# Latent heads: the softmax reciprocal moved from the probability rows to the output blocks

## The chip, the cores and the metric

One core of a Trainium2 chip runs the whole kernel as one program. The time is that of the device in microseconds (us), the median of several executions. TensorE (PE) multiplies matrices, VectorE (DVE) and ScalarE (ACT) work on tiles element by element, GpSimd (POOL) on tiles in SBUF, and SyncE (SP) issues the DMAs. The engines run side by side and wait for each other by semaphores.

## The reference

A two-layer decoder trunk on 1024 positions of width 1024: layer 0 mixes tokens by stick-breaking attention, layer 1 by latent attention (MLA) with 12 heads; both have 4 memory heads beside them, an output projection and a SwiGLU block. The change concerns the 12 latent heads of layer 1 alone. With q and k of 96 columns each and v of 64, they compute

```
sc = einsum('bhqd,bhkd->bhqk', q_blk, k) * scale
sc = where(key_pos <= q_pos, sc, -inf)
p  = softmax(sc, axis=-1)
o  = einsum('bhqk,bhkd->bhqd', p, v)
```

and o, heads side by side, goes into the output projection.

## The kernel before, in words

All matrix products are made of fp32r parts: each operand is split into an upper and a lower part, and a product is three matmuls (lines 84 to 86, `product3`). The latent heads are in `latent_heads` (line 2928 on), which builds one object `at_` of class `Attend`. It works on six pairs of heads. A pair is four jobs: head 0 with queries 0 to 511, head 0 with queries 512 to 1023, then head 1 in the same way. A job has four rows (tiles of 128 queries) and 4 or 8 blocks of 128 keys; a pair has 16 rows and 24 blocks, numbered tau.

For each row ("S") TensorE makes the scores in a bank pair of PSUM, with the causal mask added (line 2984); VectorE takes the negated maximum (line 1212) and multiplies it with the query's scale (line 1217); ScalarE makes the exponential into a row of SBUF, `p`, and the row's sum beside it ("P", line 1181). Then VectorE takes the reciprocal of the sum ("I", line 1226) and multiplies the row with it in place ("R", line 1232). For each block ("T") TensorE transposes up to four 128x128 tiles of the rows (line 1153) into one of two PSUM banks, ScalarE copies the upper part out (`pt_hi`, line 1193), VectorE subtracts to get the lower part (`pt_lo`, line 1237), and two blocks later ("V", `LAG` = 2) TensorE multiplies both with the values (lines 1165 and 1167). The values stand as upper and lower part side by side, so a job's output bank has 128 partitions: 64 of each part. At a job's end ("E") ScalarE copies the lower 64 out (`o_tmp`, line 1199) and VectorE adds them to the upper 64 (`o_out`, line 1243). There is one output bank, which the addition frees. SP stores the 64x512 tile (line 1258) to `attention_out_t` in DRAM, transposed: head columns in the partitions, queries along the tile.

The order of the steps is one list that all engines follow, written by `Attend.__init__` from `plan` (how many rows' scores are made by each block); the list wraps, so that the first rows of the next pair are made in the last blocks of this one. Between the steps ("X", `extras`) stands the preparation of the next pair: key and value products ("kv"), query products ("q"), norms ("ss", "rq", "ksum", "knorm"), key transposes ("kturn": `kt_hi` by ScalarE at line 3176, `kt_lo` by VectorE at line 3268), and weight splits ("wk", "wq"). VectorE's scaling of a query is line 3250, ScalarE's square of it line 3161, TensorE's sum of squares line 3347. All preparation products use one PSUM bank. The first pair is prepared in a list `OPENING` of its own. The last pair runs the list without the next pair's rows and without `extras` (`closing`), and ends in 36 filler matmuls (`keep_running`, line 92). SP loads the weights of the pair after next (lines 3021 and 3024) at a pair's start and then runs `at_.sync`, the four output stores of a pair, in order.

Of the kernel before, what the change touches and what calls it, by code (L numbers as in the profile page):

```python
# [1022 lines left out]
class Attend:  # L1023
# [8 lines left out]
    def __init__(self, nc, ctx, tag, mem, psum, k, jobs, keys_of, blocks_of, causal, scores, values, store,  # L1032
                 rows_mem, ring, score_banks, out_banks=(6, 7), plan=None, extras={}, lag=1, wrap=False, low_mem=None,
                 query_scale=None, stored=()):
# [14 lines left out]
        (self.scores_made, self.raw_max, self.nmax_done, self.exp_done, self.inv_done, self.rows_done,  # L1049
         self.turned, self.hi_done, self.split_done, self.pv_made, self.tmp_done, self.out_done) = (  # L1050
            ctx.semaphore(f"{tag}_{n}") for n in (
                "scores_made", "raw_max", "nmax_done", "exp_done", "inv_done", "rows_done", "turned",
                "hi_done", "split_done", "pv_made", "tmp_done", "out_done"))
# [11 lines left out]
        steps, made, exps, inverses, rows = [], 0, 0, 0, 0  # L1065
# [15 lines left out]
        def inverse_up_to(count):  # L1081
            nonlocal inverses
            exp_up_to(count)
            while inverses < count:
                steps.append(("I", inverses // 4, inverses % 4))
                inverses += 1

        def row_up_to(count):
            nonlocal rows
            inverse_up_to(count)  # L1090
            while rows < count:
                steps.append(("R", rows // 4, rows % 4))
                rows += 1

        score_up_to(plan[0])
        row_up_to(plan[0])
# [16 lines left out]
        row_up_to(plan[-1])  # L1113
# [3 lines left out]
        self.closing = [s for s in steps if s[0] not in "SPIR" or s[1] < self.nj] + (rest if wrap else [])  # L1117
# [19 lines left out]
    def pe(self, pe, steps, turn=0, extra=None, ready=None, values_ready=None):  # L1137
        for kind, *step in steps:
# [2349 lines left out]
```

## Time and profile before

| | us |
|---|---|
| three runs | 2627.41, 2628.19, 2633.21 |
| median | 2628.19 |
| the profiled execution | 2629.66 |
| its span, first to last instruction | 2627.90 |
| TensorE busy | 2526.2 (96%) |
| VectorE busy | 1739.8 (66%) |
| ScalarE busy | 1310.6 (50%) |
| GpSimd busy | 1112.5 (42%) |

The latent heads take the span's part from about 1482 to 1890 us. An engine's busy time counts its own instructions alone. Matmuls are pipelined, so their durations overlap: a 512-wide one is shown with 0.39 us and the next starts 0.23 us later. "Idle" in square brackets is the engine's gap just before an instruction, with the instruction of another engine that ended it. "PEclk" is the clock granted to TensorE, 1.00 for 2.4 GHz and 0.50 for 1.2 GHz.

### The profile page before, as it was taken

What the parts mean: (1) busy time and instruction counts of PE and PEld (TensorE: products, weight loads), DVE (VectorE), ACT (ScalarE), POOL (GpSimd) and SP (SyncE); (2) the same over time, 40 slices, a digit from 0 to 9 for tenths busy, and PEclk for the clock granted to TensorE, in tenths of its full rate; (3) what the DMA queues carried; (4) which work ended last, traced back from release to release, by engine and by line L of the source; (5) the groups of instructions that cost most, each with busy time, mean ns of one, the idle gap of its engine ahead of it and who ended that gap; (6) DMA issues with size and microseconds to landing.
All of it is one profiled execution on the core that took longest, in us unless ns stands there. A gap on an engine that the chain in (4) does not pass through costs nothing. (4 is left out here: it accounts for less than half of the span.)

```text
span 2627.9 us, 37382 instructions
## 1 busy us (share of the span) xinstructions
PE 2526.2 (96%) x12150; PEld 2057.7 (78%) x12150; DVE 1739.8 (66%) x2659; ACT 1310.6 (50%) x2483; POOL 1112.5 (42%) x839
## 2 busy tenths in 40 slices
PE   7999999999999999999989999999899999999999
PEld 6867777667888888888777777778687888888887
DVE  6767787855765666478655377777648665665595
ACT  6567777745433333444655366666545333333443
POOL 2134454311465566555411332332003665565554
PEclk9999999999999999999999999999899999999999
DMA  4111110153222232674302000000242322234843
GB/s 145 45 29 33 33 33 9 33 176 113 81 100 104 100 112 88 228 240 148 107 21 59 14 20 22 21 21 21 83 166 90 116 100 104 100 112 143 285 125 117
DMA packets 182796, 242.76 MB, mean 92 GB/s; under 512 B 31376, under 2 KB 105872, under 8 KB 182672
## 3 DMA queue, kind: packets, MB, share of 16 engines
q1 hardware_dynamic: 182672, 241.19, 27.7%
q8 instruction: 68, 1.11, 0.2%
q14 instruction: 56, 0.46, 0.1%
HBM read 175.60 MB, written 65.54 MB: 92 GB/s over the span
## 5 line engine op out<-in xcount | busy, mean ns | idle before, releaser
L2385 POOL TENSOR_TENSOR l0s_run_lo<-l0s_run,l0s_run_hi 128x512 fp32r<-128x512 f32 (+2 forms) x120 | 143.5, 1195 | 215.6 <-DVE l0s_run_hi L2538 215.6
L477 POOL TENSOR_TENSOR l1f_wd_lo<-l1f_d,l1f_wd_hi 128x512 fp32r<-128x512 f32 x77 | 108.0, 1403 | 104.6 <-ACT l1f_wd_hi L552 104.6
L477 POOL TENSOR_TENSOR l0f_wd_lo<-l0f_d,l0f_wd_hi 128x512 fp32r<-128x512 f32 x77 | 109.3, 1422 | 97.2 <-ACT l0f_wd_hi L552 97.0
L84 PE MATMUL banks<-l1f_T_hi,l1f_op_hi 128*128 128x512 f32 x352 | 137.1, 390 | 1.1 <-DVE l1f_T_lo L697 1.1
L84 PE MATMUL banks<-l0f_T_hi,l0f_op_hi 128*128 128x512 f32 x352 | 137.1, 390 | 1.0 <-DVE l0f_T_lo L697 1.0
L85 PE MATMUL banks<-l0f_T_lo,l0f_op_hi 128*128 128x512 f32 x352 | 137.0, 389 | 0.0
L85 PE MATMUL banks<-l1f_T_lo,l1f_op_hi 128*128 128x512 f32 x352 | 136.9, 389 | 0.0
L86 PE MATMUL banks<-l1f_T_hi,l1f_op_lo 128*128 128x512 f32 x352 | 136.9, 389 | 0.0
L86 PE MATMUL banks<-l0f_T_hi,l0f_op_lo 128*128 128x512 f32 x352 | 136.9, 389 | 0.0
L439 POOL TENSOR_TENSOR l1f_s<-l1f_raw 128x512 f32<-128x512 f32 x44 | 66.6, 1513 | 158.1 <-DMA l1f_raw<-in_w_ffn_gu_dram 135.3
L509 ACT ACTIVATE l1f_op_hi<-l1f_s 128x512 fp32r<-128x512 f32 x88 | 55.2, 631 | 140.4 <-PE banks L86 140.4
L509 ACT ACTIVATE l0f_op_hi<-l0f_s 128x512 fp32r<-128x512 f32 x88 | 55.2, 631 | 140.4 <-PE banks L86 140.4
L462 POOL TENSOR_TENSOR l1f_hid<-l1f_c,l1f_gate 128x512 f32<-128x512 f32 x44 | 67.5, 1535 | 129.6 <-DVE l1f_c L719 129.6
L462 POOL TENSOR_TENSOR l0f_hid<-l0f_c,l0f_gate 128x512 f32<-128x512 f32 x44 | 67.0, 1524 | 129.5 <-DVE l0f_c L719 129.5
L84 PE MATMUL banks<-ht_hi,l0s_w_hi 128*128 128x512 f32 x288 | 119.6, 415 | 1.4 <-DVE l0s_q L2033 1.2
L84 PE MATMUL banks<-l0f_wd_hi,l0f_a_hi 128*128 128x512 f32 x308 | 120.0, 390 | 0.6 <-DVE l0f_a_lo L760 0.6
L439 POOL TENSOR_TENSOR l0f_s<-l0f_raw 128x512 f32<-128x512 f32 x44 | 66.5, 1512 | 127.0 <-DMA l0f_raw<-in_w_ffn_gu_dram 102.9
L1237 DVE TENSOR_TENSOR l1aa_pt_lo<-banks,l1aa_pt_hi 128x512 fp32r<-128x512 f32 (+2 forms) x144 | 78.8, 554 | 62.3 <-ACT l1aa_pt_hi L1193 61.9
L86 PE MATMUL banks<-l0f_wd_hi,l0f_a_lo 128*128 128x512 f32 x308 | 119.8, 389 | 0.0
L85 PE MATMUL banks<-l0f_wd_lo,l0f_a_hi 128*128 128x512 f32 x308 | 119.8, 389 | 0.0
L84 PE MATMUL banks<-l1f_wd_hi,l1f_a_hi 128*128 128x512 f32 x308 | 119.8, 389 | 0.0
L85 PE MATMUL banks<-l1f_wd_lo,l1f_a_hi 128*128 128x512 f32 x308 | 119.8, 389 | 0.0
(536 smaller groups left out, 8456.1 us busy)
## 6 DMA issues: line engine op xcount, KB each, us to landing
l0f_raw<-in_w_ffn_gu_dram SPq DMA_DIRECT2D x22, 1024.0 KB, 5.0
l1f_raw<-in_w_ffn_gu_dram SPq DMA_DIRECT2D x22, 1024.0 KB, 4.9
l0f_a_raw<-hidden_rows SPq DMA_DIRECT2D x77, 256.0 KB, 3.9
l1f_a_raw<-hidden_rows SPq DMA_DIRECT2D x77, 256.0 KB, 3.4
hidden_rows<-l0f_hid SPq DMA_DIRECT2D x44, 256.0 KB, 2.0
l0f_d<-in_w_ffn_down_dram SPq DMA_DIRECT2D x44, 256.0 KB, 4.9
hidden_rows<-l1f_hid SPq DMA_DIRECT2D x44, 256.0 KB, 2.0
l1f_d<-in_w_ffn_down_dram SPq DMA_DIRECT2D x44, 256.0 KB, 4.8
```

The costliest lines, as they stand in the source:

```text
L84: pe.matmul(out, l_hi, r_hi, start=first, stop=False, skip_group_check=True)
L85: pe.matmul(out, l_hi, r_lo, start=False, stop=False, skip_group_check=True)
L86: return pe.matmul(out, l_lo, r_hi, start=False, stop=last, skip_group_check=True)
L439: pool.tensor_tensor(out[:], left, right, op).then_inc(s_made, 1)
L462: pool.tensor_tensor(hidden(q), cs[q][:], gate[q][:], ALU.mult).then_inc(hid_done, 1)
L477: pool.tensor_tensor(wd_lo[g % RING][:], held[HELD_AT[DOWN[p][1]]][i][:], as_f32(wd_hi[g % RING][:]), ALU.subtract).then_inc(wd_lo_done, 1)
L509: act.activation(op_hi[n][:], stationary(n, b), ACT.Copy).then_inc(op_hi_done, 1)
L1237: dve.tensor_tensor(self.pt_lo[tau % self.np][:, c0:HALF], self.t_ps[tau % 2][:, c0:HALF], as_f32(self.pt_hi[tau % self.np][:, c0:HALF]), ...
L2385: pool.tensor_tensor(run_lo[x % NR][:, f:HALF], run[x % NR][:, f:HALF], as_f32(run_hi[x % NR][:, f:HALF]), ALU.subtract).then_inc(run_spli ...
```

## The change

The probability rows stay unscaled. The four sums of a job are inverted in one instruction (128x4) after the first score of the next job, SP stores them to a DRAM tensor `row_scales` as 512 values in the order of the queries, and loads that row back into 64 partitions (`o_scale`). At a job's end VectorE adds the two parts of the output as before, into `o_sum`, and then multiplies with `o_scale` into `o_out`. The transposes wait for the exponentials and no longer for the scaled rows. `rsum`, `rinv`, `o_scale` and `o_out` have two buffers each. The first two jobs' scales are sent (`first_scales`) ahead of the second pair's weights; later SP's order is, for job n: store its reciprocals, store the output of job n - 2, load its scales.

```diff
-        self.nmx, self.rsum, self.rinv, self.raw_nmx = (low_mem(f"{tag}_{n}", [P, 4])
-                                                        for n in ("nmx", "rsum", "rinv", "raw_nmx"))
-        self.o_tmp = mem(f"{tag}_o_tmp", [HD, HALF])
-        self.o_out = [mem(f"{tag}_o_out{s}", [HD, HALF]) for s in range(2)]
+        self.nmx, self.raw_nmx = (low_mem(f"{tag}_{n}", [P, 4]) for n in ("nmx", "raw_nmx"))
+        self.rsum, self.rinv = ([low_mem(f"{tag}_{n}{s}", [P, 4]) for s in range(2)] for n in ("rsum", "rinv"))
+        parts, both = mem(f"{tag}_parts", [P, HALF]), [mem(f"{tag}_out_scale{s}", [P, HALF]) for s in range(2)]
+        self.o_tmp, self.o_sum = parts[0:HD, :], parts[HD:2 * HD, :]
+        self.o_out, self.o_scale = [t[0:HD, :] for t in both], [t[HD:2 * HD, :] for t in both]
...
         def score_up_to(count):
             nonlocal made
             while made < count:
                 exp_up_to(made)
-                row_up_to(made - 1)
                 steps.append(("S", made // 4, made % 4))
                 made += 1
+                if made % 4 == 1 and made > 4:
+                    steps.append(("I", made // 4 - 1))
...
-                row_up_to(max(rows, 4 * n + 4))
-                inverse_up_to(exps - 1)
+                exp_up_to(max(exps, 4 * n + 4))
                 steps.append(("T", n, j, tau))
...
-                pe.wait_ge(self.rows_done, turn * self.ns + 4 * n + 4)
+                pe.wait_ge(self.exp_done, turn * self.ns + 4 * n + 4)
...
+                if i == 0 and (n >= 2 or not (isinstance(turn, int) and turn == 0)):
+                    act.wait_ge(self.inv_done, turn * self.nj + n - 1)
...
-                dve.reciprocal(self.rinv[:, one], self.rsum[:, one]).then_inc(self.inv_done, 1)
-            elif kind == "R":
-                n, i = step
-                s = 4 * n + i
-                one, row = slice(s % 4, s % 4 + 1), self.p[n % self.ring][i]
-                dve.wait_ge(self.inv_done, turn * self.ns + s + 1)
-                dve.tensor_scalar(row[:], row[:], self.rinv[:, one], None, ALU.mult).then_inc(self.rows_done, 1)
+                n = step[0]
+                dve.wait_ge(self.exp_done, turn * self.ns + 4 * n + 4)
+                if n >= 2 or not (isinstance(turn, int) and turn == 0):
+                    dve.wait_ge(self.scale_stored, 16 * (turn * self.nj + n - 1))
+                dve.reciprocal(self.rinv[n % 2][:], self.rsum[n % 2][:]).then_inc(self.inv_done, 1)
...
                 dve.wait_ge(self.tmp_done, turn * self.nj + n + 1)
+                dve.tensor_tensor(self.o_sum, self.o_ps[n % len(self.o_ps)][0:HD, :], self.o_tmp, ALU.add).then_inc(self.out_done, 1)
+                dve.wait_ge(self.out_done, 1 + turn * self.nj + n + 1)
                 dve.wait_ge(self.stored[n % 2], 16 + 16 * (turn * (self.nj // 2) + n // 2))
-                dve.tensor_tensor(self.o_out[n % 2][:], self.o_ps[n % len(self.o_ps)][0:HD, :], self.o_tmp[:],
-                                  ALU.add).then_inc(self.out_done, 1)
+                dve.wait_ge(self.scale_in[n % 2], 16 * (turn * (self.nj // 2) + n // 2 + 1))
+                dve.tensor_tensor(self.o_out[n % 2], self.o_sum, self.o_scale[n % 2], ALU.mult).then_inc(self.out_scaled, 1)
...
+    def store_scale(self, sp, n, turn=0):
+        sp.wait_ge(self.inv_done, turn * self.nj + n + 1)
+        with self.nc.allow_non_contiguous_dma("row scales"):
+            sp.dma_start(self.scale_dram[n % self.nj].rearrange("(i p) -> p i", p=P), self.rinv[n % 2][:]).then_inc(self.scale_stored, 16)
+
+    def load_scale(self, sp, n, turn=0):
+        sp.wait_ge(self.scale_stored, 16 * (turn * self.nj + n + 1))
+        sp.dma_start(self.o_scale[n % 2], self.scale_dram[n % self.nj].partition_broadcast(HD)).then_inc(self.scale_in[n % 2], 16)
...
+    def first_scales(self, sp):
+        for n in range(2):
+            self.store_scale(sp, n)
+            self.load_scale(sp, n)
+
+    def sync(self, sp, turn=0, last=False):
+        for n in range(2, self.nj if last else self.nj + 2):
+            self.store_scale(sp, n, turn)
+            self.store_out(sp, n - 2, turn)
+            self.load_scale(sp, n, turn)
+        if last:
+            for n in range(self.nj - 2, self.nj):
+                self.store_out(sp, n, turn)
...
             load(1)
+            at_.first_scales(sp)
             with sp.Fori(0, PAIRS - 2) as g:
                 load(g + 2)
                 at_.sync(sp, g)
```

## Rows read from the trace of the kernel before

**Rows 1.** Busy time by stretch: us, each engine (x instructions), granted clock, DMA, GB/s

```profile
1500.00:1540.00 40.00, 34.93 (x208) 29.27 (x205) 28.09 (x68) 23.56 (x57) 15.22 (x15) 1.00 0.09 22
1540.00:1840.00 300.00, 284.63 (x1689) 236.94 (x1688) 237.14 (x570) 199.31 (x468) 82.96 (x86) 1.00 0.08 20
1840.00:1895.00 55.00, 43.00 (x222) 35.73 (x221) 36.30 (x79) 28.04 (x58) 1.27 (x1) 0.81 0.16 49
```

**Rows 2.** TensorE's waits, 1540 to 1840: us in total, times, longest

```profile
PE banks L3347 <- DVE l1a_kt_lo L3268: 4.5, 5, 1.0
PE banks L3347 <- ACT l1a_q_sq L3161: 3.5, 5, 0.7
PE banks L3364 <- DVE l1a_kt_lo L3268: 2.5, 5, 0.5
PE banks L84 <- ACT l1aa_p L1181: 2.3, 4, 0.6
```

**Rows 3.** Groups, 1500 to 1895: busy us, mean ns of one, idle before

```profile
L1232 DVE TENSOR_SCALAR l1aa_p<-l1aa_p,l1aa_rinv 128x128 f32<-128x128 f32 (+3 forms) x96 | 53.8, 565 | 2.3
...
L1243 DVE TENSOR_TENSOR l1aa_o_out<-banks,l1aa_o_tmp 64x512 f32<-64x512 f32 x24 | 16.3, 679 | 1.5 <-ACT l1aa_o_tmp L1199 1.2
...
L1226 DVE RECIPROCAL l1aa_rinv<-l1aa_rsum 128x1 f32<-128x1 f32 x96 | 14.7, 153 | 3.3 <-ACT l1aa_p L1181 3.3
...
L3244 DVE TENSOR_TENSOR l1a_k<-l1a_k,l1a_rk 128x512 f32<-128x512 f32 x11 | 7.6, 692 | 0.4
```

**Rows 4.** Timeline of a middle pair: start us, us, instruction, idle before

```profile
1770.18 0.74 DVE L3268 SCALAR_TENSOR_TENSOR l1a_kt_lo<-banks,l1a_gcol,l1a_kt_hi 128x512 fp32r<-128x512 f32 x1
...
1770.97 1.08 PE L3347 MATMUL banks<-l1a_q_sq,l1a_ones 128*64 128x512 f32 x4 [0.98 <-DVE l1a_kt_lo L3268]
```

**Rows 5.** Timeline, second block of a pair

```profile
1785.69 0.67 DVE L3250 TENSOR_TENSOR l1a_q<-banks,rope_table 128x512 f32<-128x512 f32 x1
```

**Rows 6.** Timeline, end of the opening

```profile
1527.11 2.53 DVE L1232 TENSOR_SCALAR l1aa_p<-l1aa_p,l1aa_rinv 128x1024 f32<-128x1024 f32 x2
...
1530.39 0.41 PE L1153 MATMUL banks<-ident,l1aa_p 128*128 128x128 f32 x2 [1.91 <-DVE l1aa_pt_lo L1237]
```

**Rows 7.** Timeline, start of the last pair

```profile
1846.10 0.93 DVE L1232 TENSOR_SCALAR l1aa_p<-l1aa_p,l1aa_rinv 128x1024 f32<-128x1024 f32 x2
...
1847.78 0.66 PE L1153 MATMUL banks<-ident,l1aa_p 128*128 128x128 f32 x2 [2.79 <-DVE l1aa_pt_lo L1237]
```

**Rows 8.** Timeline, last pair, before its last two jobs' blocks

```profile
1870.26 0.19 ACT L1181 ACTIVATION_READ_ACCUMULATOR l1aa_p<-banks,l1aa_nmx,l1a_rq 128x1 f32 x1
...
1870.28 0.47 PE L1165 MATMUL banks<-l1aa_pt_hi,l1a_v 128*128 128x512 f32 x1 [2.24 <-DVE l1aa_pt_lo L1237]
...
1872.22 1.11 PE L1153 MATMUL banks<-ident,l1aa_p 128*128 128x128 f32 x4 [0.66 <-DVE l1aa_p L1232]
```

**Rows 9.** Busy time and granted clock in stretches of the last pair and the opening

```profile
1843.55:1847.80 4.25, 0.71 (x6) 0.64 (x6) 3.53 (x13) 3.63 (x8) 0.00 (x0) 0.94 0.00 0
1847.80:1854.10 6.30, 5.95 (x24) 5.28 (x25) 2.87 (x7) 2.33 (x7) 1.27 (x1) 0.50 0.60 191
1867.80:1871.30 3.50, 1.26 (x8) 0.74 (x6) 3.43 (x8) 2.69 (x6) 0.00 (x0) 0.98 0.00 0
1871.30:1881.20 9.90, 8.44 (x32) 6.84 (x32) 4.45 (x10) 3.69 (x7) 0.00 (x0) 0.50 0.11 26
1527.00:1530.50 3.50, 1.59 (x8) 1.01 (x8) 3.47 (x5) 1.38 (x3) 3.50 (x3) 1.00 0.07 26
```

**Rows 10.** DMA issues: count, KB each, median us from issue to landing

```profile
attention_out_t<-l1aa_o_out SPq DMA_DIRECT2D x24, 128.0 KB, 2.2
...
l1m_mcol<-in_ln_mem_dram SPq DMA_DIRECT2D x1, 4.0 KB, 3.8
...
l0m_gcol<-in_ln_attn_dram SPq DMA_DIRECT2D x1, 4.0 KB, 12.6
```

**Rows 11.** Timeline, end of the stage

```profile
1884.30 4.51 PE L92 MATMUL banks<-strict,ident_r 128*128 128x256 f32 x36
```

More of the change, by code:

```diff
@@ L1064, in __init__ @@
                           for j in range(blocks_of(half))]
-        steps, made, exps, inverses, rows = [], 0, 0, 0, 0
+        steps, made, exps = [], 0, 0
         def score_up_to(count):
@@ L1079, in exp_up_to @@
                 exps += 1
[L1081 to L1093, printed above, removed]
         score_up_to(plan[0])
-        row_up_to(plan[0])
+        exp_up_to(plan[0])
         self.opening, steps = steps, []
@@ L1112, in __init__ @@
             steps += rest
-        row_up_to(plan[-1])
+        exp_up_to(plan[-1])
         self.steps = steps
         self.first_steps = [s for s in steps if s[0] not in "VE" or s[1] >= 0]
-        self.closing = [s for s in steps if s[0] not in "SPIR" or s[1] < self.nj] + (rest if wrap else [])
+        self.closing = [s for s in steps if s[0] not in "SPI" or s[1] < self.nj] + (rest if wrap else [])
     def product(self, tau):
@@ L1253, in begin, with store_out @@
             sp.sem_inc(s, 16)
-    def sync(self, sp, turn=0):
-        for n, (h, half) in enumerate(self.jobs):
-            sp.wait_ge(self.out_done, 1 + turn * self.nj + n + 1)
-            sp.dma_start(self.store(h, half, turn), self.o_out[n % 2][:]).then_inc(self.stored[n % 2], 16)
+    def store_scale(self, sp, n, turn=0):
[5 more added lines that the diff above has]
+        sp.dma_start(self.o_scale[n % 2], self.scale_dram[n % self.nj].partition_broadcast(HD)).then_inc(self.scale_in[n % 2], 16)
+    def store_out(self, sp, n, turn=0):
+        h, half = self.jobs[n]
+        sp.wait_ge(self.out_scaled, turn * self.nj + n + 1)
+        sp.dma_start(self.store(h, half, turn), self.o_out[n % 2]).then_inc(self.stored[n % 2], 16)
+    def first_scales(self, sp):
[10 more added lines that the diff above has]
+                self.store_out(sp, n, turn)
     def stores(self, turns):
@@ L2925, in _, with latent_heads @@
             last.then_inc(ss_made, 1)
-def latent_heads(nc, tag, k, w_q_up, w_kv_up, g_k, cq, ckv, table, k_rot, k_ss, q_eps, at, psum, ot_dram, passage, w_out, stored, opening):
+def latent_heads(nc, tag, k, w_q_up, w_kv_up, g_k, cq, ckv, table, k_rot, k_ss, q_eps, at, psum, ot_dram, scale_dram, passage, w_out, stored, opening):
     mem = Memory(nc, at, 229344)
@@ L2989, in latent_heads @@
                      lambda h, half, g: ot_dram[bass.ds(g * P + h * HD, HD), half * HALF:(half + 1) * HALF],
-                     low, 4, psum["pair"], (6,), plan, extras, LAG, True, mem, lambda h, tile: rq[:, NS * h + tile:NS * h + tile + 1], stored)
+                     low, 4, psum["pair"], (6,), plan, extras, LAG, True, mem, lambda h, tile: rq[:, NS * h + tile:NS * h + tile + 1], stored, scale_dram)
         sem = lambda n: ctx.semaphore(f"{tag}_{n}")
@@ L3052, in _ @@
             load_passage(sp, passage, w_out, ot_dram, passage_in)
-            at_.sync(sp, PAIRS - 1)
+            at_.sync(sp, PAIRS - 1, True)
             sp.wait_ge(passage_in, 64)
@@ L3457, in build @@
                 heads_count = latent_heads(nc, f"{tag}a", k, a["mla_w_q_up"][0], a["mla_w_kv_up"][0], a["mla_g_kn"][0],
-                             cq, ckv, table, k_rot, k_ss, q_eps, mem.at, psum, ot_dram, passage, a["w_out"][layer], kept[6:8], opening)
+                             cq, ckv, table, k_rot, k_ss, q_eps, mem.at, psum, ot_dram, scale_dram, passage, a["w_out"][layer], kept[6:8], opening)
             project_and_swiglu(nc, f"{tag}f", k, x, x_dram, x_att, a_dram, ot_dram, a["w_out"][layer], a["ln_ffn"][layer],
```

20 lines of the change are left out of this document (10 added, 10 removed).

## The prediction

> **What bounds the kernel now.** I read the busy table of the stage that the change touches first, by stretches. The twelve latent heads run as six pairs, from 1500 to 1890 us. In 1540 to 1840 (five pairs less a little) TensorE is busy 284.63 of 300 us, VectorE 237.14, ScalarE 199.31 [rows 1]. So TensorE sets the pace, and all that a lighter VectorE can give there is TensorE's idle time, 15.4 us in all. The opening (1500 to 1540) has 5.1 us of it, the last stretch (1840 to 1895) 12.0 us, and only the last runs at a mean granted clock of 0.81 [rows 1].
>
> Next the list of waits, to see how much of the idle time ends on VectorE. In 1540 to 1840 TensorE waited 4.5 us for the split of the keys (kt_lo), 3.5 us for the squared queries, 2.5 us again for kt_lo and 2.3 us for an exponential that frees a score bank [rows 2]: 12.8 of the 15.4 us, or about 2.6 us a pair. Two of the four end directly on VectorE, the other two stand one step behind it (the exponential needs the row maximum, the square needs the scaled query).
>
> The groups of instructions then say what the change takes away. Scaling the probability rows costs VectorE 53.8 us in 96 instructions, the 96 reciprocals 14.7 us [rows 3].
>
> **The change part by part.**
>
> *VectorE's load.* Removed: 53.8 us of row scaling, and 96 reciprocals of 153 ns become 24, so 72 x 0.153 = 11.0 us. Added: one multiplication of 64x512 per job, 24 in all. The trace has none like it. The nearest rows are the addition that it follows, 64x512 in 679 ns, and a multiplication of two tiles in SBUF, 128x512 in 692 ns [rows 3]; I take 0.69 us, plus 0.08 for waiting on its own engine's addition, so 24 x 0.77 = 18.5 us. The upper bound is the slowest case beside GpSimd's work that I saw: a pair of row scalings (1024 and 128 wide) took 2.53 us in the opening [rows 6] and 0.93 us where GpSimd was idle [rows 7], 1.6 us more, which would make it 2.3 us. The lower bound is half a full-width operation, 0.35 us, if partitions counted. Net, VectorE loses 53.8 + 11.0 - 18.5 = 46 us, nearly 8 us a pair. None of that is time by itself, since TensorE sets the pace; it counts only where TensorE waits.
>
> *The transposes' new wait.* They waited for the scaled rows and now wait for the exponentials, one VectorE step earlier. ScalarE's and TensorE's order of work does not change; ScalarE's new wait, for a reciprocal two jobs back, is met long before.
>
> *Middle pairs (five).* I took the stalls one at a time. The longest: a row's scaling (565 ns by the mean of all widths [rows 3]) stands in front of the row maximum that delays kt_lo to 1770.18, and TensorE stands 0.98 us [rows 4]. Without it kt_lo starts 0.3 to 0.6 us earlier: take 0.4. The other kt_lo stall (0.5 us a pair) has a scaling in front in the same way: it goes. The stall on the exponential (2.3 / 4 = 0.57 us) has one in front too: 0.45. The one on the squared query (0.7 us) lies behind VectorE work that stays: half, 0.35. The small stall at a bank that the output addition frees: 0.15. That is 1.85 us a pair. What is late next: in the second block of a pair the multiplication now stands between the output addition and the scaling of a query (0.67 us, at 1785.69 [rows 5]); the query's square follows, 0.6 us on ScalarE, and then the key product that takes its bank. The path has about 0.3 us to spare, so some 0.4 us of new stall. And 0.25 us a pair for stalls that only move to the next wait. 1.85 - 0.4 - 0.25 = 1.2 us a pair, 6.0 us for five. Bounds: 0 (all moves on) and 2.6 us a pair (13 us).
>
> *Opening.* At the start of the first block the two scalings of 2.53 us hold back the splits, and TensorE stands 1.91 us at 1530.39 [rows 6]. Without them the first split follows its upper part directly, before TensorE has run out of query products: all 1.9 us. The other gaps there belong to the chain of the query norms, of which VectorE's rows are a small part: 0.3. Together 2.2 us; bounds 1.0 and 3.0.
>
> *Last pair.* Here TensorE has no preparation of a next pair to fill with. At its start two scalings (0.93 us) stand before the splits, and TensorE idles 2.79 us to 1847.78 [rows 7]. Without them the splits follow ScalarE's two exponentials and its upper parts, 1.1 us earlier; a shorter stall just ahead gives 0.4. Later TensorE idles 2.24 us to 1870.28. The row names the split, but the product also needs the output bank, which the output addition (0.67 us) freed just before. Of this only 0.35 us of that is the scaling of a row, the rest is the maximum of the last 1024-wide row. Then the transposes wait for the last row's scaling until 1872.22, though its exponential was read out at 1870.26 + 0.19 [rows 8]. They now queue only behind the two products before them, and start near 1870.9: 1.3 us with the 0.35. Sum 1.1 + 0.4 + 1.3 = 2.8, less 0.1 for the multiplication in front of a later split: 2.7 us. Bounds 1.5 and 4.
>
> *The clock in the last pair.* It fell to its lower level (0.50, 1.2 GHz) twice: for 6.3 us from 1847.8 and for 9.9 us from 1871.3. Ahead of the falls TensorE was busy 0.71 of 4.25 us and 1.26 of 3.50 us; in a stretch of the opening with 1.59 of 3.50 us it stayed at 2.4 GHz [rows 9]. Without the removed waits the first stretch would hold about 1.7 us idle at a time, less than the opening's 1.91; the second still about 1.9. So I expect the first fall to go (chance 0.65) and the second to go or shorten in half the cases. Worth: in the first stretch TensorE was busy 5.95 us, at double rate 3.0, but the split chain takes part of it: 2.0 us. In the second the blocks came every 1.7 us and would come every 0.95 (one upper part of 0.6 and one split of 0.69 us, two banks deep): 3.2 us. I put 2.0 + 1.0 = 3.0 us into the sum; bounds 0 and 5.2. The Trainium skill (TensorE: Matmul & The Clock Gate, Terms) prices a throttled stretch at its length times the missing share of the clock; by that rule the two stretches cost 3.2 and 4.9 us, and the sum would be 5.1 us larger. The rows speak for less, since in such a stretch TensorE also waits for the splits.
>
> *The trip through DRAM.* Per job a store of 512 separate 4-byte values and a load of 512 values into each of 64 partitions, both on SP's queue. The nearest rows: a load of 1024 single values landed after 3.8 us [rows 10], output stores of the same 128 KB as the new load after 2.2 us; with two issues of 0.5 us, 7 us. The slowest small load of the page, behind other traffic, took 12.6 us [rows 10]: 16 us as the upper bound. A job's sums are complete at the first score of the next job, its product ends eight or more blocks later: at least 20 us in the middle pairs, about 11 us for the third job of the last pair. So it is hidden. SP waits longer before it stores an output tile, which nobody waits for within that time. The weights of the second pair are issued behind the first two trips, 7 us later, near 1532, and are used after 1542. The Trainium skill speaks against this edit (DMA: Bandwidth & Descriptors, Rules for kernel authors: a strided last dimension becomes one descriptor per element, and should be rearranged). It changes no number here, because the trip's length is covered.
>
> *End of the stage.* The last output tile is ready 0.8 us later. TensorE's 36 filler products run from 1884.30 to 1888.81 [rows 11], and the next stage starts only behind them; the addition ended at 1885.8, so 3 us of cover: nothing.
>
> **Sum.** 6.0 + 2.2 + 2.7 + 3.0 = 13.9 us. The profiled execution took 2629.66 us (span 2627.9 and 1.8 around it), so 2615.8. It lay 1.5 us above the median of the three runs, 2628.19, so I predict 2614.3.
>
> **Rivals.**
> A. *The clock does not come back* (both gaps are still long enough, or fall so that they count). For it: the second gap stays near 1.9 us. Against it: the opening's row. Gain 13.9 - 3.0 = 10.9 us: 2617.3.
> B. *The waits only move.* TensorE is already 95% busy in the middle pairs, and each stall has ScalarE's work behind it too (exponential, upper part, square). The middle gives 0 to 1, opening and last pair 2 to 3: about 2624.
> C. *The multiplication lies on the path*: slower. VectorE runs in order, so at each job's end the next split or row maximum waits 0.77 us more; if TensorE follows each time, 24 x 0.77 = 18.5 us against 13.9 gained, or 2633. It decides from 0.58 us exposed per job. Against it: four jobs a pair lose 16 scalings in exchange, and the splits have slack of a block in most places.
> D. *The scales come too late*: a trip of over 20 us stalls VectorE, and behind it TensorE. At 25 us, 5 us for each of some 20 jobs: +86 us, 2714. No row is near.
>
> **How the numbers follow.** Forecast (gain 9 to 20 us, with one or both falls of the clock gone or shortened): 0.60. A: 0.17. B: 0.16. C: 0.05. D: 0.02. Single runs of this kernel differ by up to 0.2% (5.3 us), about what can be told from no change. Half of B gains less than that, and a fifth of C loses less. Faster by over 0.2%: 0.60 + 0.17 + 0.08 = 0.85; within: 0.08 + 0.01 = 0.09; slower: 0.04 + 0.02 = 0.06. Range: A and most of B are inside, and the upper bounds of middle and clock at the low end: 2606 to 2623.5.
>
> **What would show it.** Row scalings gone, 24 reciprocals of 128x4, 24 multiplications of 0.69 us. VectorE's busy time in the stage down by some 46 us. In the list of waits kt_lo and the exponential at half their times; the gap at the start of the first block gone; the transposes of the last job starting right after the products before them; mean clock of the last stretch above 0.9. VectorE never waiting for a landed scale. Wrong would be: a multiplication well over 0.7 us, a new wait of the key product for the squared query over 0.5 us a pair, or the same clock in the last stretch.

## The result, and the profile after

The changed kernel takes 2640.95 us (median of 6 runs, 2636.28 to 2644.97), the one before 2627.78 (6 runs beside them, 2624.93 to 2633.21). The ratio is 1.0049, 95% interval 1.0035 to 1.0063: 0.5% slower, where 0.5% faster was predicted. The profiled execution took 2642.17 us with a span of 2640.4, which is 12.5 us more than the span before.

To place these 12.5 us I cut the stage at instructions that every kernel of this study has: VectorE's first memset (the stage starts), ScalarE's copies of the upper half of the output (one per job, 24 in all), and ScalarE's first instruction of the next stage. "Opening" runs to the first copy, "five pairs" to the 21st, "last pair" to the 24th. All in us. The four columns of the stage come from one execution of each kernel, the profiled one; the medians are of all runs. The kernel before was timed again beside each group of experiments, and its medians there lie between 2629.2 and 2631.0, so kernels of different groups are best compared by their ratios. The cut "last pair" leaves out the first 11 us or so of the last pair, which fall under "five pairs". In "multiply, no trip" two memsets of the ones stand ahead of the instruction that is taken as the start.

| kernel | opening | five pairs | last pair | stage | median |
|---|---|---|---|---|---|
| before | 55.21 | 316.99 | 30.11 | 407.89 | 2627.78 |
| after | 55.50 | 323.44 | 34.96 | 419.58 | 2640.95 |
| rows unscaled only | 54.60 | 307.52 | 25.80 | 393.52 | 2613.04 |
| multiply, no trip | 51.87 | 322.84 | 27.41 | 407.73 | 2629.99 |
| trip, no multiply | 55.40 | 312.64 | 35.16 | 408.87 | 2628.93 |
| compact store | 55.55 | 322.59 | 27.43 | 411.25 | 2632.17 |
| multiply deferred | 55.30 | 310.11 | 37.23 | 408.32 | 2628.76 |
| compact, strided read | 53.05 | 331.25 | 27.36 | 417.34 | 2637.60 |
| deferred and compact | 53.05 | 308.69 | 28.90 | 396.32 | 2617.41 |
| GpSimd multiplies | 53.05 | 312.59 | 27.74 | 399.04 | 2619.57 |
| behind next split, compact | 54.59 | 315.15 | 28.14 | 403.55 | 2628.94 |
| pair-crossing one deferred | 55.50 | 316.87 | 36.56 | 414.61 | 2632.83 |

So 11.7 of the 12.5 us lie in this stage: 6.45 in the five pairs, 4.85 in the last one. The busy table of the changed kernel, to be held against [rows 1] (us, each engine's busy time, granted clock, DMA share, GB/s):

```profile
1500.00:1540.00 40.00, 35.77 (x202) 29.68 (x201) 20.85 (x48) 24.30 (x58) 15.42 (x16) 0.96 0.03 4
1540.00:1840.00 300.00, 278.24 (x1646) 231.49 (x1645) 217.51 (x446) 190.25 (x453) 80.81 (x86) 1.00 0.14 31
1840.00:1895.00 55.00, 39.73 (x224) 33.18 (x223) 35.02 (x70) 30.87 (x66) 2.58 (x2) 0.88 0.21 50
```

In 1540 to 1840 VectorE has 20 us less to do and TensorE, which should have gained from it, stands 6.4 us longer. TensorE's waits in that stretch (us in total, times, longest), against [rows 2]:

```profile
PE banks L3359 <- DVE l1a_kt_lo L3280: 6.0, 4, 1.5
PE banks L84 <- ACT l1a_q_sq L3173: 5.9, 4, 1.5
PE banks L3359 <- ACT l1a_q_sq L3173: 4.0, 5, 1.2
PE banks L84 <- ACT l1a_v L3165: 2.4, 5, 0.5
PE banks L1154 <- DVE l1aa_parts L1228: 1.7, 8, 0.5
PE banks L3376 <- ACT l1a_q_sq L3173: 1.3, 4, 0.4
```

The wait for an exponential is gone, as forecast, and so is the second one for kt_lo. The second line is new and is the largest change: a key product (line 84) waits 1.5 us in each pair for a squared query. The third job's end has the same chain in front of the key transposes (the last line). The first line, 4.5 us before, and the third, 3.5 before, have grown. The second block of a pair shows where it comes from (start us, duration, engine, instruction, idle before it):

```profile
1595.88 0.69 DVE L1228 TENSOR_TENSOR l1aa_parts<-banks,l1aa_parts 64x512 f32<-64x512 f32 x1
...
1596.45 1.28 POOL L3073 TENSOR_TENSOR l1a_v<-l1a_v,l1a_v 128x512 fp32r<-128x512 f32 x1 [10.04 <-ACT l1a_v L3201]
...
1596.81 1.47 DVE L1232 TENSOR_TENSOR l1aa_out_scale<-l1aa_parts,l1aa_out_scale 64x512 f32<-64x512 f32 x1 [0.25 <-DVE l1aa_parts L1228]
...
1598.31 0.69 DVE L3262 TENSOR_TENSOR l1a_q<-banks,rope_table 128x512 f32<-128x512 f32 x1
...
1599.12 0.60 ACT L3173 ACTIVATE l1a_q_sq<-banks 128x512 f32<-128x512 f32 x1 [2.74 <-DVE l1a_q L3262]
...
1599.77 0.38 PE L84 MATMUL banks<-l1a_wk_hi,ckv_hi 128*128 128x256 f32 x1 [1.47 <-ACT l1a_q_sq L3173]
```

Read it backwards: TensorE idles 1.47 us for the square; the square started when the query was scaled; the scaling stood behind the new multiplication, which waited 0.25 us for VectorE's own addition and then took 1.47 us where the same instruction takes 0.69 us in three jobs of four. A subtraction of GpSimd runs from 1596.45 to 1597.73, and the multiplication ends 0.55 us behind it. The kernel before had this to spare at the same place:

```profile
1785.69 0.67 DVE L3250 TENSOR_TENSOR l1a_q<-banks,rope_table 128x512 f32<-128x512 f32 x1
1786.48 0.60 ACT L3161 ACTIVATE l1a_q_sq<-banks 128x512 f32<-128x512 f32 x1 [1.04 <-DVE l1a_q L3250]
...
1787.34 0.33 PE L84 MATMUL banks<-l1a_wk_hi,ckv_hi 128*128 128x256 f32 x1
```

The square ended at 1787.08, 0.26 us before the key product. The multiplication puts in 0.25 + 1.47 = 1.72 us, and 1.72 - 0.26 = 1.46 is the wait that is measured. The Trainium skill has the mechanism (SBUF — State Buffer, SBUF: two separate sides): a VectorE instruction with two inputs in SBUF and a GpSimd instruction that reads SBUF exclude each other, and whichever starts first holds the shared ports to its end. The trace agrees.

In the last pair the time goes to one wait:

```profile
1871.15 0.38 SPq L1246 DMA_DIRECT2D row_scales<-l1aa_rinv  x1
...
1882.31 0.45 SPq L1250 DMA_DIRECT2D l1aa_out_scale<-row_scales  x1
...
1882.81 0.59 SPq L1246 DMA_DIRECT2D row_scales<-l1aa_rinv  x1
...
1883.75 0.69 DVE L1228 TENSOR_TENSOR l1aa_parts<-banks,l1aa_parts 64x512 f32<-64x512 f32 x1
...
1890.85 0.69 DVE L1232 TENSOR_TENSOR l1aa_out_scale<-l1aa_parts,l1aa_out_scale 64x512 f32<-64x512 f32 x1 [6.42 <-DMA l1aa_out_scale<-row_scales]
...
1892.41 1.09 PE L1142 MATMUL banks<-ident,l1aa_p 128*128 128x128 f32 x4 [6.24 <-DVE l1aa_pt_lo L1223]
```

The scales of the third job leave at 1871.15; the load behind them can only be issued at 1882.31, when the store has landed, and VectorE goes on 8.5 us later. The trip takes 19.7 us. Most trips of this trace take about 13 us from store to landed load, with a load of 2.7 to 5.2 us; in three of 24, of which this is the last, the load takes 8.1 to 9.8 us. All three loads have the next job's store, 512 single numbers, issued 0.5 to 2 us behind them, but four others with such a store 0.6 us behind landed after 2.7 to 2.8 us. So that store alone is not the reason, and what makes three of the loads long is open; with the compact store (below) none took over 4.1 us. VectorE stands for 6.42 us, behind it the splits, behind them TensorE. The clock in this stretch (columns as above):

```profile
1876.00:1886.20 10.20, 6.76 (x34) 5.27 (x32) 5.86 (x11) 5.88 (x13) 0.00 (x0) 0.83 0.20 27
1886.20:1892.40 6.20, 0.00 (x0) 0.02 (x1) 1.52 (x3) 0.15 (x1) 0.00 (x0) 0.72 0.03 0
1892.40:1898.00 5.60, 5.59 (x25) 4.50 (x26) 2.43 (x5) 1.95 (x5) 0.00 (x0) 0.71 0.14 47
```

The groups of 1500 to 1900, against [rows 3] (busy us, mean ns of one, idle before):

```profile
L1208 DVE TENSOR_TENSOR l1aa_nmx<-l1aa_raw_nmx,l1a_rq 128x1 f32<-128x1 f32 x96 | 31.0, 323 | 5.0
...
L1232 DVE TENSOR_TENSOR l1aa_out_scale<-l1aa_parts,l1aa_out_scale 64x512 f32<-64x512 f32 x24 | 20.4, 849 | 9.6 <-DMA l1aa_out_scale<-row_scales 6.4 <-DVE l1aa_parts L1228 2.8
...
L1218 DVE RECIPROCAL l1aa_rinv<-l1aa_rsum 128x4 f32<-128x4 f32 x24 | 4.2, 176 | 4.2 <-ACT l1aa_p L1172 1.9 <-issue 1.5 <-DMA row_scales<-l1aa_rinv 0.8
```

### The profile page after: what moved, and what is told of

Same layout as the page of the kernel before. It is cut to its first block and busy times, and to the rows that moved or that the text cites. A ratio compares the mean times of both kernels' runs of the same rounds, so it can differ in the third digit from the quotient of the medians.

```text
span 2640.4 us, 37367 instructions
## 1 busy us (share of the span) xinstructions
PE 2524.9 (96%) x12150; PEld 2056.4 (78%) x12150; DVE 1718.0 (65%) x2515; ACT 1310.1 (50%) x2483; POOL 1112.3 (42%) x839
## 3 DMA queue, kind: packets, MB, share of 16 engines
q1 hardware_dynamic: 197264, 244.39, 28.1%
## 5 line engine op out<-in xcount | busy, mean ns | idle before, releaser
L86 PE MATMUL banks<-l1f_wd_hi,l1f_a_lo 128*128 128x512 f32 x308 | 119.8, 389 | 0.0
```

Of the source, the lines that this page charges most:

```text
L86: return pe.matmul(out, l_lo, r_hi, start=False, stop=last, skip_group_check=True)
```

## The experiments

All were timed over five rounds beside the kernel before. In the first four kernels one part each is taken out of the change. The edits are cut to the lines that matter; "..." marks what is left out.

**Rows unscaled only.** The rows are no longer scaled, and the output is not normalised at all: no multiplication, no trip.

```diff
-                dve.tensor_tensor(self.o_sum, self.o_ps[n % len(self.o_ps)][0:HD, :], self.o_tmp, ALU.add).then_inc(self.out_done, 1)
-                dve.wait_ge(self.out_done, 1 + turn * self.nj + n + 1)
                 dve.wait_ge(self.stored[n % 2], 16 + 16 * (turn * (self.nj // 2) + n // 2))
-                dve.wait_ge(self.scale_in[n % 2], 16 * (turn * (self.nj // 2) + n // 2 + 1))
-                dve.tensor_tensor(self.o_out[n % 2], self.o_sum, self.o_scale[n % 2], ALU.mult).then_inc(self.out_scaled, 1)
+                dve.tensor_tensor(self.o_out[n % 2], self.o_ps[n % len(self.o_ps)][0:HD, :], self.o_tmp, ALU.add).then_inc(self.out_done, 1)
...
```

> Leaves the normalisation out: rows unscaled, no multiplication of the output block, no trip through DRAM; the reciprocals (24 of 128x4) stay. Theory Q (the removed row scaling does give what was forecast without the clock; the multiplication in VectorE's queue and the trip cost more): 8 to 14 us below before, about 2617. Theory M (waits only move, ScalarE's and TensorE's own order bound the pairs): 0 to 4 us below before, 2624 to 2628; the intervals between the same job ends of successive middle pairs stay at 63.5 to 63.9 us, while by Q they fall to about 62.

Measured: 2613.04 us (2609.51 to 2618.22), ratio 0.9943 [0.9930, 0.9957]. A pair takes 62.2 us instead of 63.8, and the "last pair" of the table 25.8 instead of 30.1. Removing the row scaling is worth what was forecast for the whole change; everything that is lost comes from what was put in its place.

**Multiply, no trip.** The multiplication stays, by a tile of ones written once; the output is not normalised.

```diff
-                dve.wait_ge(self.scale_in[n % 2], 16 * (turn * (self.nj // 2) + n // 2 + 1))
...
+            for t in at_.o_scale:
+                dve.memset(t, 1.0)
```

> As the changed kernel, but the output blocks are multiplied with a constant tile of ones, and no reciprocal goes to DRAM. Theory Q1 (the multiplication stands in front of the scaling of a query, and with two SBUF operands it waits for GpSimd): middle pairs as in the changed kernel, 65.7 us from job end to job end, the 1.5 us wait of the key product for the squared query still there; the last pair's 6.2 us stall gone: 2633 to 2636. Theory Q2 (the trip's small packets and SP's order cost the middle pairs too): middle pairs back at 63.7 or less, 2622 to 2627.

Measured: 2629.99 us, ratio 1.0002 [0.9992, 1.0011]. The multiplication alone costs 17 us over the kernel without it: 15.3 in the five pairs, 1.6 in the last. A middle pair takes 65.4 us, close to theory Q1's 65.7, and the key product's 1.5 us wait is there; the total lies below Q1's range and above Q2's. Of the 1.6 us, 1.4 lie between the second and the third output copy, where the granted clock is 0.72 in the mean, against 1.00 without the multiplication.

**Trip, no multiply.** Store, load and VectorE's wait for the load stay; the addition writes the output block itself, the multiplication is a copy of one column, and the output is not normalised.

```diff
-                dve.tensor_tensor(self.o_out[n % 2], self.o_sum, self.o_scale[n % 2], ALU.mult).then_inc(self.out_scaled, 1)
+                dve.tensor_copy(self.o_sum[:, 0:1], self.o_scale[n % 2][:, 0:1]).then_inc(self.out_scaled, 1)
```

> As the changed kernel, but the output block isn't multiplied (one column of the loaded scales is copied instead, so that VectorE's wait for them stays). Theory Q1: middle pairs at 62 to 64 us, the 6 us stall in the last pair stays: 2622 to 2630. Theory Q2: middle pairs at 65 to 66, 2636 to 2641.

Measured: 2628.93 us, ratio 0.9997 [0.9986, 1.0008]. The last pair takes 35.16 us, 9.4 more than with neither, and a middle pair about 63 us; both this and the total lie where theory Q1 put them. The five pairs take 5.1 us more too; yet with the multiplication in place the trip adds only 0.6 there (323.44 against 322.84). The two costs don't add up in the middle pairs, and which of wait, copy and traffic makes the 5.1 us was not separated.

**Compact store.** The scales are stored as 128 runs of 16 bytes; they reach the wrong queries.

```diff
-            sp.dma_start(self.scale_dram[n % self.nj].rearrange("(i p) -> p i", p=P), self.rinv[n % 2][:])...
+            sp.dma_start(self.scale_dram[n % self.nj].rearrange("(p i) -> p i", i=4), self.rinv[n % 2][:])...
```

> As the changed kernel, but the reciprocals are stored with the four values of a partition side by side in DRAM (128 runs of 16 bytes in place of 512 of 4), which gives the scales to the wrong queries. If the store's 10 us come from the number of runs, it falls to 3 to 4 us, the next load lands in under 4 us too, and the last pair's wait of 6.4 us for a landed scale goes: 6 us below the changed kernel, 2635. If the time is the round trip of any small store, nothing moves: 2641.

Measured: 2632.17 us, ratio 1.0008 [0.9996, 1.0020]. The last pair takes 27.43 us, as without any trip; the middle pairs don't move (65.6 us against 65.7). The median is 8.8 us below the changed kernel's, where 6 were expected. SP's wait for its store in 1500 to 1895 (us in total, times, longest), in the changed kernel:

```profile
SPq L1250 <- DMA row_scales<-l1aa_rinv: 159.3, 21, 10.2
```

and with the compact store:

```profile
SPq L1250 <- DMA row_scales<-l1aa_rinv: 11.9, 19, 1.7
```

With the multiplication in place, the trip costs nothing in either part once it is short (322.59 and 27.43 us, against 322.84 and 27.41 without a trip). It left the question of why 24 multiplications cost 17 us.

**Multiply deferred.** The multiplication gets a step of its own at the end of the block.

```diff
                 steps += [("X", x) for x in extras.get(tau, ())]
+                steps += [("M", s[1]) for s in self.product(tau - lag)[1:]]
```

> The multiplication of a job stands behind the extras of its block in VectorE's order, not right behind the addition; all else as changed. Theory (it costs time because of where it stands: at the second block of a pair it is ahead of the query scaling, on which TensorE's key product waits): the stretch from one pair's last output copy to the next pair's first falls from 9.85 to about 8.4 us, a middle pair from 65.7 to about 64.2, the last pair stays near 35 (the trip is not touched), total about 2631. Rival (VectorE's busy time bounds these stretches, wherever the multiplication stands): a middle pair stays at 65.7, total about 2640.

Measured: 2628.76 us (12 runs), ratio 0.9992 [0.9977, 1.0007]. The direction is the theory's, the size is not: a middle pair takes 62.35 us, 3.3 less, not 1.5. The stretches between the four output copies of a pair went from 24.86, 10.48, 20.48 and 9.86 us to 24.09, 10.46, 19.60 and 8.19: three of the four places had a price, not one. The second block was only the one that showed as a single long wait. (Of the five intervals between the pairs' first copies, the first and the fourth take 63.19 and 63.03 us.) The last pair still has its long wait for the scales, 9.1 us in this trace, and takes 37.23 us, 2.3 more than in the changed kernel; why it is longer was not followed.

**Compact, strided read.** A store in 16-byte runs that is right for each query: the multiplication reads the scales with a step of four numbers.

```diff
+                four = lambda t: t.rearrange("d (i p) -> d i p", p=P)
+                dve.tensor_tensor(four(self.o_out[n % 2]), four(self.o_sum),
+                                  self.o_scale[n % 2].rearrange("d (p i) -> d i p", i=4), ALU.mult)...
```

> The scales are stored as 128 runs of 16 bytes and loaded as they lie; the multiplication reads them with a step of four numbers, so that each query gets its own. Theory (the last pair lost its time to the store of 512 single numbers): the last pair falls from 35.0 to about 27.4 us, a middle pair stays at 65.6, total about 2632, as in the run with the compact store. Rival (reading one of two inputs with a step of 16 bytes slows the multiplication, say to 1.4 us each, 4 a pair on the path as the plain one is): a middle pair at 67 to 68 us, total 2640 to 2645.

Measured: 2637.60 us (2635.57 to 2642.39), ratio 1.0036 [1.0023, 1.0049]. The last pair fell as expected, but the rival's size came true in the middle, 68.0 us a pair (the total lies between the two forecasts). The first of its multiplications:

```profile
1535.39 1.09 DVE L1233 TENSOR_TENSOR l1aa_out_scale<-l1aa_parts,l1aa_out_scale 64x512 f32<-64x512 f32 x1
```

1.09 us in place of 0.69, and 1.85 in place of 1.46 beside GpSimd's subtraction. The Trainium skill (SBUF — State Buffer, Door 1: The DMA port swizzle) says that full rate needs a second access within the same 16 bytes; here each number of the scales lies in another 16, and the trace agrees. A multiplication longer by 0.4 us, four times a pair, made the pair 2.35 us longer: where it stands, each microsecond of it costs more than one.

**Deferred and compact.** The last two edits together.

> Both edits together: the multiplication behind the block's extras, the compact store with the strided read. Theory (two independent losses): middle pair 64.2, last pair 27.4, total about 2623, faster than the kernel before by 0.2 to 0.3%. Rival (VectorE's time bounds, place does not matter): about 2632, no difference from the compact store alone.

Measured: 2617.41 us (2613.08 to 2623.90), ratio 0.9962 [0.9946, 0.9977]. It computes all that the change computes and is 0.4% faster than the kernel before, where the changed kernel is 0.5% slower. A middle pair takes 62.4 us, against 62.2 with no multiplication at all, though three of a pair's four now take 1.08 us and the fourth 1.36. The last pair takes 28.9 us, 3.1 more than with none; 2.1 of them lie between its second and third copy, at a mean granted clock of 0.75 against 1.00. Both theories' totals were too high. The same place as above:

```profile
1586.17 1.28 POOL L3078 TENSOR_TENSOR l1a_v<-l1a_v,l1a_v 128x512 fp32r<-128x512 f32 x1 [10.02 <-ACT l1a_v L3206]
1586.32 0.69 DVE L3267 TENSOR_TENSOR l1a_q<-banks,rope_table 128x512 f32<-128x512 f32 x1
...
1587.04 1.35 DVE L1236 TENSOR_TENSOR l1aa_out_scale<-l1aa_parts,l1aa_out_scale 64x512 f32<-64x512 f32 x1
1587.12 0.60 ACT L3178 ACTIVATE l1a_q_sq<-banks 128x512 f32<-128x512 f32 x1 [1.03 <-DVE l1a_q L3267]
```

The query scaling, which reads one input from PSUM, runs at its usual 0.69 us beside GpSimd; the square starts right behind it, and the stretched multiplication has nobody behind it. TensorE's waits in 1540 to 1840, with the key product's gone:

```profile
PE banks L3364 <- DVE l1a_kt_lo L3285: 5.2, 5, 1.2
PE banks L3364 <- ACT l1a_q_sq L3178: 3.5, 5, 0.7
PE banks L1143 <- DVE l1aa_pt_lo L1224: 2.3, 2, 2.1
```

**GpSimd multiplies.** Compact store; the multiplication is four more steps of GpSimd, which waits for its own instruction before and behind each.

```diff
-    POOL_ORDER = ("v1", "ksq 0", "ksq 1", "krot 0", "qlo 0", "qlo 1", "krot 1", "qlo 2", "wq 0", "wq 1", ...
+    POOL_ORDER = ("v1", "m -1", "ksq 0", "m 0", "ksq 1", "krot 0", "qlo 0", "qlo 1", "krot 1", "m 1", "qlo 2", "wq 0", "m 2", "wq 1", ...
```

> The compact store, and the multiplication moved from VectorE to GpSimd, which does it between its own subtractions and waits for its instruction before and behind it; the addition of a job waits until the job before is multiplied. Theory (what costs is VectorE's part of the multiplication, with the wait for its own addition ahead of it): a middle pair falls to about 62.5 to 63, as without the multiplication, total about 2618 to 2620. Rival (GpSimd's multiplication, over 1.3 us each, holds VectorE up while it runs, or delays GpSimd's subtractions on which key products wait): a middle pair at 65 us or above, total 2630 or above.

Measured: 2619.57 us (2617.76 to 2621.16), ratio 0.9963 [0.9950, 0.9976]; a middle pair 63.5 us. The total is the theory's, the middle pair half a microsecond above its range. The group of its multiplications in 1540 to 1840:

```profile
L1239 POOL TENSOR_TENSOR l1aa_out_scale<-l1aa_parts,l1aa_out_scale 64x512 f32<-64x512 f32 x18 | 27.8, 1546 | 73.9 <-DVE l1aa_parts L1230 48.0 <-issue 24.6 <-POOL l1a_v L3080 1.1
```

1.55 us each, against 1.08 for VectorE's with the same read, and yet the five pairs are only 5.1 us longer than without any multiplication (312.59 against 307.52), a third of what VectorE's 0.69 us cost right behind the addition. This run takes the work off VectorE and changes its place at once, so it does not tell the two apart.

**Behind next split, compact.** As deferred and compact, but the multiplication stands behind the split of the next block.

```diff
                 steps.append(("T", n, j, tau))
+                steps += [("M", s[1]) for s in self.product(tau - lag - 1)[1:]]
```

> As the run with both edits (deferred multiplication, compact store), but the multiplication stands one step later still: behind the split of the next block, not ahead of it. Theory (in the last pair, where no extras lie between, the multiplication still delays that split: its last pair took 28.9 us against 25.8 with no multiplication at all): middle pair stays at 62.4, the last pair falls to about 27, total about 2615.5. Rival (what is left in the last pair is the state of the clock or the longer strided read, not the place): last pair stays at 28 to 29, total 2617 to 2618.

Measured: 2628.94 us (12 runs), ratio 0.9996 [0.9985, 1.0008]. This theory fell: the last pair gave 0.8 us, not 1.9, and at 28.1 lies where the rival put it, with a mean clock of 0.73 between its second and third copy, where it was 0.75 before this edit and 1.00 with no multiplication. The middle pairs lost 1.3 each (63.7 us), in three of the four stretches. The traces say in whose way the multiplication now is. It starts just ahead of a subtraction of GpSimd twice a pair, and these take 1.38 and 2.12 us where they take 1.04 and 1.42 alone: here GpSimd is the one that waits. TensorE's waits grow from 5.2 to 9.0 us for kt_lo, and from 0.7 to 3.1 for the output addition (all of 1540 to 1840). Which of the two begins the loss is not shown.

**Pair-crossing one deferred.** Of the four multiplications of a pair only the one in the second block of the next pair is deferred; store and load as changed.

```diff
+                steps += [("M", s[1]) for s in self.product(tau - lag)[1:] if s[1] == -1]
```

> Only the multiplication of a pair's fourth job, which falls into the second block of the next pair, is deferred behind that block's extras; the three others and the trip stay as changed. Theory (each place has its own price, 1.66 us here, 0.8 and 0.9 at the first and third job, nothing at the second, as the stretches of the run with all four deferred show against the changed kernel): a middle pair at 64.0, total about 2633 to 2634. Rival (the 3.3 us a pair come from this place alone, by what it sets off in later blocks): a middle pair at 62.4, total as with all four deferred, 2629.

Measured: 2632.83 us (12 runs), ratio 1.0010 [0.9999, 1.0021]; a middle pair 64.0 us. The theory holds. Each place has its own price: 1.65 us here, and 24.85 and 20.47 us in the stretches behind the first and third job's copies, untouched by this edit.

## Why the prediction was wrong, by its own steps

*Row scaling removed: right in sum, not in its parts.* Without multiplication and trip the kernel gained 14.4 us in the stage. The forecast without what it took off for the multiplication (2.0 and 0.1) is 16.0, of which the clock in the opening hid some. The middle pairs gave about 1.65 us each, where the stalls of [rows 2] and [rows 4] promised 1.6 (1.85 less 0.25). But the longest stall, from which 0.4 us a pair was to come, did not move; with the rows unscaled only it still reads

```profile
PE banks L3348 <- DVE l1a_kt_lo L3269: 4.5, 5, 1.1
```

as before. The waits for the exponential and the second one for kt_lo went whole. That the sum came out is in part luck.

*Opening: right, and hidden by the clock.* Forecast 2.2 us. In the kernel with deferred multiplication and compact store it is 55.21 - 53.05 = 2.16. The 13 us from 40 to 53 us behind the stage's start, first in the kernel before:

```profile
1522.19:1535.19 13.00, 11.02 (x69) 9.30 (x68) 9.49 (x22) 6.78 (x17) 6.66 (x7) 1.00 0.17 43
```

then in the deferred and compact kernel, where the 1.91 us of [rows 6] is gone:

```profile
1518.06:1531.06 13.00, 12.92 (x85) 11.42 (x84) 6.79 (x17) 8.05 (x21) 6.53 (x8) 1.00 0.32 76
```

and in the changed kernel's profiled execution, as free of gaps, but at a granted clock of 0.88:

```profile
1523.90:1536.90 13.00, 12.92 (x71) 11.11 (x70) 6.06 (x17) 7.43 (x19) 7.13 (x7) 0.88 0.07 12
```

Such a fall stands in seven of the eleven traces without row scaling (mean clock of their openings 0.92 to 0.94; 0.97 or 0.98 in the other four and in the one trace of before). So it may belong to the change and not to chance; no run decides it.

*The multiplication in the middle pairs: the step that failed.* The prediction said that its path "has about 0.3 us to spare, so some 0.4 us of new stall", in one of a pair's four jobs, and nothing in the others: 2.0 us in all. It measured 15.3 us, 3.1 a pair. The 0.3 us to spare was right, though no row was given for it: it is 0.26. Three errors are in the rest. The instruction was taken as 0.77 us, with 0.08 for the wait that no row shows and that measures 0.22 to 0.25; in the job that counts it was 0.25 + 1.47, because GpSimd was at work, although the bound of 2.3 us had been read off just such a case [rows 6] and was used for the load only, not for the stall. The third job's end has the same query scaling behind it and was not looked at. And the first job's end has a price of 0.8 us as well, by a chain that I did not follow. That the place makes most of the price is shown: deferred by a few instructions, the same multiplications leave a middle pair at 62.35 us against 62.2 (the five pairs at 310.1 against 307.5, the long store included). GpSimd's part is smaller: it makes one multiplication of four 0.78 us longer (1.47 less 0.69), by estimate 0.8 of the 3.1 us a pair. The prediction had named this failure among its signs, a new wait of the key product for the squared query over 0.5 us a pair; it is 1.5.

*Last pair and clock: near in sum, wrong in its parts.* Forecast 2.8 + 3.0 = 5.8 us without the multiplication. The prediction thought that the first fall of the clock would go (0.65) and that the second might. With the rows unscaled only it was the other way round. The gap at the start of the last pair shrank from 2.79 to 2.06 us, not to 1.7, and the fall behind it stayed:

```profile
1831.93:1833.99 2.06, 0.00 (x1) 0.03 (x1) 1.01 (x3) 2.04 (x7) 0.00 (x0) 0.99 0.00 0
1834.00:1840.60 6.60, 6.25 (x25) 5.58 (x26) 2.89 (x7) 3.05 (x8) 1.27 (x1) 0.50 0.64 209
```

None of the eleven traces without row scaling is free of it (mean clock 0.53 to 0.75 between the fourth copy of the fifth pair and the first of the last). The second fall went whole, and with it the table's "last pair" gave 4.3 us. The start gave about 1.2 us, the excess of the fifth of the five intervals (2.8) over a middle pair's 1.65, where 1.5 of waits and 2.0 of clock were forecast. The multiplication was priced at 0.1 us there and cost 1.6, mostly because the second fall comes back with it (0.72 against 1.00, above). In the changed kernel the stretch from 1840 to 1895 ran at 0.88, below the 0.9 that was named as a sign.

*The trip: the second step that failed.* Forecast 7 us, upper bound 16, covered everywhere. It took 13 us in most jobs and 19.7 us where it mattered. The nearest row chosen [rows 10] was a load of single numbers in 3.8 us; a store of single numbers took about 10. The forecast's own cover for the third job of the last pair, 11 us, was below its own upper bound, and that was the place to stop. The stall cost 7.55 us (34.96 - 27.41). The sentence of the Trainium skill that spoke against this edit (DMA: Bandwidth & Descriptors, Rules for kernel authors: one descriptor per element of a strided last dimension) was cited and set aside as covered; the last pair was decided by it. The trace agrees with it: packets under 512 bytes grew by 13056, and by 3840 with 16-byte runs. The weights behind the first two trips are those of the third pair, not the second; they went out at 1539.52 where 1532 was forecast, and no wait of TensorE for them is in the lists.

*VectorE's load.* Forecast 46 us less. By the groups: -53.8 for the rows, -10.5 for the reciprocals, +20.4 for the multiplications, and +6.9 on the small multiplications that make the maxima (24.1 before, 31.0 after). -37 us. The 6.9 are GpSimd's: in the kernel before 20 of the 96 started while GpSimd was at work and took 11.9 us together, in the changed one 19 did and took 18.7, and the others took 0.16 each in both. And -37 is the sum of the records, which overlap each other a little. The time in which VectorE ran anything, from the stage's start to its last output copy, fell from 301.8 to 278.6 us, by 23: half of what was forecast. A sum of records overstates what an engine is freed of.

*The account.* Forecast -13.9, measured +11.7 in the stage, 25.6 apart: multiplication in the five pairs 13.3, in the last 1.5; trip 7.55 and 0.6; clock in the opening of this execution 2.45. The last pair's gain came 1.5 short in the table's cut and the five pairs' 1.5 better, since its start is counted with them; these cancel. The 0.2 us that are left lie in roundings and the stage's end.

*Rivals.* C was the right one in kind: the multiplication lies on the path. Its size, 24 x 0.77 = 18.5 us if TensorE follows each time, is near the 16.9 measured by luck, since the four places of a pair cost 0.8, 0, 0.9 and 1.65 us and not 0.77 each. It had 0.05, because "four jobs a pair lose 16 scalings in exchange": but the scalings had been spread over the stage and the multiplication is concentrated in front of the step that a chain waits for. D's mechanism came true too, once in 24 jobs instead of some 20 times. B is refuted by the rows unscaled only: the middle gave far more than 0 to 1 us. A was half right: one of the two falls stayed.

## What to carry to other kernels

Work that is halved in total can still cost time if the rest is put in front of the one instruction that another engine waits for; price an added instruction at each of its places by what stands behind it in its queue, with its slowest observed duration, and put it behind those. Here the 24 instructions cost 17 us right behind the addition and about 4 a few instructions later (1.2 in the five pairs and 3.1 in the last, with a slower read of the scales and a short trip). A transfer that is "hidden" has to be held, at its upper bound, against the shortest cover in the whole stage, which is at its end, where no next piece of work is left to stretch it.

## What the runs showed of the hardware that was not expected

A store of 512 single 4-byte values from 128 partitions kept the load that needs it waiting up to 10.2 us, and 7.8 to 11.5 us passed from the issue of one to that of the other; 128 runs of 16 bytes landed after 1.4 us (median). Three loads of 128 KB among the former took 8.1 to 9.8 us, against a median of 3.8; the longest among the latter took 4.1.

A VectorE instruction with both inputs in SBUF waits for a running GpSimd instruction even if it is tiny. Of the 96 small multiplications of the changed kernel (128x1), 77 took 0.16 us; the 19 that started under a GpSimd instruction took 0.86 to 1.42 us, and every one of them ended within 0.02 us of it. This one, 128x1, took 0.86 us and ended with GpSimd's, which ran from 1646.16 to 1647.58; at 1601.53, with GpSimd idle, it took 0.16:

```profile
1646.16 1.42 POOL L3082 TENSOR_TENSOR l1a_wq_lo<-l1a_wq_raw,l1a_wq_hi 128x576 fp32r<-128x576 f32 x1 [6.29 <-ACT l1a_wq_hi L3150]
...
1646.73 0.86 DVE L1208 TENSOR_TENSOR l1aa_nmx<-l1aa_raw_nmx,l1a_rq 128x1 f32<-128x1 f32 x1
```

Reading one of two fp32 inputs with a step of 16 bytes made a 64x512 multiplication take 1.08 us in place of 0.69.

Of 17 executions of the kernel before in one set, those at a mean granted clock of 0.990 took 2626.7 to 2629.6 us and the four at 0.987 took 2636.3 to 2636.7: the time goes with the clock, and a difference of 5 us needs its stage read from the trace, with the clock of each part beside it, and not the medians alone.
